# GpSimd sums the depthwise convolution's products four tiles at a time and completes conv_y itself, in a decoder trunk

## The chip, the cores and the metric

The kernel runs on one core of a Trainium2 chip (trn2). The metric is the device time of one execution, in microseconds; where several executions were timed, their median. PE is TensorE, DVE VectorE, ACT ScalarE, POOL GpSimd, SP SyncE.

## The reference, cut to what matters

One step of a two-layer trunk over 320 tokens (256 of a prompt, 8 samples of 8), with 2048 features. Layer 0 begins with a Conformer convolution module; it is the only part in which the change works on new data:

```python
def causal_dwconv(u, prev, w, bias):
    ext = jnp.concatenate([prev.astype(u.dtype), u], axis=1)
    y = lax.conv_general_dilated(ext, w[:, None, :].astype(u.dtype), window_strides=(1,), padding='VALID',
                                 dimension_numbers=('NWC', 'WIO', 'NWC'), feature_group_count=u.shape[-1])
    return y + bias, ext[:, -(w.shape[0] - 1):]

def conformer_conv(x, prev, w_in, b_in, w_dw, b_dw, g_n, b_n, w_out, b_out):
    a, gate = jnp.split(x @ w_in + b_in, 2, axis=-1)
    u = a * jax.nn.sigmoid(gate)
    u, new_prev = causal_dwconv(u, prev, w_dw, b_dw)
    u = jax.nn.silu(layer_norm(u, g_n, b_n))
    return u @ w_out + b_out, new_prev
```

The convolution has 31 taps per feature. Its result is normalised over the features, projected by w_out and added to DN_ALPHA * x. After it come a convolutional FFN, and in layer 1 window attention and another FFN; all of these are projections of the same kind.

## The kernel before, in words

Features lie on the 128 partitions, tokens on the free axis: x is xr[128, 16, 320]. Everything is float32. Each projection splits weights and activations into a high part (rounded to fp32r) and a low part, and sums three matmuls per 128x128 weight block: hi*hi, hi*lo, lo*hi (lines 377 to 379). Weights come by DMA from SP in half-groups ("chunks") of 128x1024 into four slots of w_raw, each as long as the longest chunk of a later stage (1408 columns); ScalarE rounds a chunk into w_hi (split_hi, line 685), VectorE writes w_lo = w_raw - w_hi (split_lo, line 991). A group is two chunks, 48 matmuls, and gives one feature tile of 128x320 in acc[0] or acc[1].

The w_in stage has 32 groups in 16 pairs ip; a pair gives the sigmoid input and the value of feature tile i. For each tile ScalarE takes the sigmoid (line 765), VectorE multiplies (gate, line 1093) into u_pad, ScalarE copies u_pad and the history into the overlapping segments u_seg (lines 783 to 785). Then the 31 taps are shared out: VectorE does 18 (lines 1102 to 1112), alternating between two PSUM banks sc[0] and sc[1]; ScalarE writes 13 products prods[:, n] (line 795), which GpSimd adds one by one into taps_pool, starting from minus the mean of tile 0 ("shift"; line 311). VectorE joins the three sums into conv_y (join, lines 1131 and 1133), but only in the next turn of the loop, after gate and the splits. For the last tile TensorE sums the products with an identity matmul (line 496), and ScalarE copies the sum to taps_pool (line 817). TensorE adds conv_y and its square (conv_square, line 708) to the moments of the norm (lines 466 and 472) two pairs late.

The order on each engine is the order of the code; all dependencies are semaphores written out by hand. ScalarE's turn is: sigmoid, four weight splits, wait for gate, u_seg, issue of the DMA that saves the state, 13 products (each waiting until GpSimd has taken the product of the tile before), a scaling of xr by ALPHA plus b_out (line 800), the square of the tile before. VectorE's turn is: two splits, gate, two splits, join of the tile before, 18 taps. SP's queue holds the weight loads, each waiting for the split of the chunk before in its slot. After tile 0 GpSimd issues three DMAs. In the norm that follows, GpSimd subtracts the mean from tiles 4 to 15 in three instructions of four tiles (center, line 329) while VectorE works on the others (lines 1021 and 1044). In the w_out stage VectorE adds the projection to xr (lines 1157, 1190 and 1196) and sums moments.

## Time and profile before

| | us |
|---|---|
| median of 3 runs | 2750.94 (2749.96 to 2757.99) |
| profiled execution: span | 2757.9 |
| the slowest of the three runs, beside that span | 2757.99 |
| TensorE busy in it | 2620.5 |
| VectorE, ScalarE, GpSimd busy | 1493.9, 1166.3, 274.9 |

The span is from the first to the last instruction of one profiled execution. Busy times of the other engines than TensorE are averages over very different stages; the w_in stage is the first 315 us, the w_out stage ends near 450 us. A row of the timeline gives the start, the duration (or, where equal instructions are merged, from the first start to the last end), the engine, the line, what is written and read, and in brackets the engine's idle time before it with the releaser.

### The profile page before, as it was taken

What the parts mean: (1) busy time and instruction counts of PE and PEld (TensorE: products, weight loads), DVE (VectorE), ACT (ScalarE), POOL (GpSimd) and SP (SyncE); (2) the same over time, 40 slices, a digit from 0 to 9 for tenths busy, and PEclk for the clock granted to TensorE, in tenths of its full rate; (3) what the DMA queues carried; (4) which work ended last, traced back from release to release, by engine and by line L of the source; (5) the groups of instructions that cost most, each with busy time, mean ns of one, the idle gap of its engine ahead of it and who ended that gap; (6) DMA issues with size and microseconds to landing.
All of it is one profiled execution on the core that took longest, in us unless ns stands there. A gap on an engine that the chain in (4) does not pass through costs nothing.

```text
span 2757.9 us, 48858 instructions
## 1 busy us (share of the span) xinstructions
PE 2620.5 (95%) x17562; PEld 2570.7 (93%) x17562; DVE 1493.9 (54%) x2187; ACT 1166.3 (42%) x1939; POOL 274.9 (10%) x224
## 2 busy tenths in 40 slices
PE   8889697999999999999989989899999999999996
PEld 7888597999999999999978979899999999999996
DVE  6888756544443344454466755654444334444555
ACT  7777635443332333343345433353343223443332
POOL 4888401000000000000010000100000000000001
PEclk9999798999999999999999968999999999999998
DMA  8444243444454344445433312434445434444542
GB/s 271 116 117 127 65 152 99 148 148 152 151 169 146 128 152 149 147 157 177 142 127 112 107 47 97 139 114 148 147 147 174 151 132 144 146 151 151 169 148 78
DMA packets 115061, 382.38 MB, mean 139 GB/s; under 512 B 29472, under 2 KB 29856, under 8 KB 114720
## 3 DMA queue, kind: packets, MB, share of 16 engines
q1 hardware_dynamic: 95328, 373.20, 41.4%
q0 software_dynamic: 992, 6.25, 0.6%
q10 hardware_dynamic: 18688, 2.21, 0.6%
q8 instruction: 34, 0.56, 0.1%
q14 instruction: 19, 0.16, 0.0%
HBM read 375.32 MB, written 8.27 MB: 139 GB/s over the span
## 4 chain that ended last, share of the span: by engine, by line
PE 85%; POOL 8%; DVE 3%; ACT 2%; issue 1%; POOLq 0%; DMA 0%; ACTq 0%; DVEq 0%; SPq 0%
PE acc L377 26%; PE acc L379 26%; PE acc L378 26%; POOL taps_pool L311 8%; PE acc L403 1%; PE acc L404 1%; PE acc L405 1%; DVE xr L1021 1%; ACT xr L728 1%; PE ot L665 0%; PE ot L667 0%; PE pt L564 0%; DVE rows L1034 0%; ACT xh L732 0%; PE pt L496 0%
## 5 line engine op out<-in xcount | busy, mean ns | idle before, releaser
L377 PE MATMUL acc<-xh,w_hi 128*128 128x320 f32 x3968 | 1236.1, 312 | 27.0 <-DVE w_lo L991 25.7
L379 PE MATMUL acc<-xh,w_lo 128*128 128x320 f32 x3968 | 1230.1, 310 | 0.0
L378 PE MATMUL acc<-xl,w_hi 128*128 128x320 f32 x3968 | 1229.7, 310 | 0.0
L685 ACT CAST w_hi<-w_raw 128x1024 fp32r<-128x1024 f32 (+1 forms) x648 | 699.0, 1117 | 556.2 <-PE acc L379 529.0
L991 DVE TENSOR_TENSOR w_lo<-w_raw,w_hi 128x1024 fp32r<-128x1024 f32 (+1 forms) x648 | 828.5, 1318 | 158.6 <-ACT w_hi L685 158.6
L377 PEld LDWEIGHTS acc<-xh,w_hi 128*128 128x128 f32 x3968 | 748.5, 189 | 41.9 <-DVE w_lo L991 32.4
L378 PEld LDWEIGHTS acc<-xl,w_hi 128*128 128x128 f32 x3968 | 748.6, 189 | 0.4
L379 PEld LDWEIGHTS acc<-xh,w_lo 128*128 128x128 f32 x3968 | 748.2, 189 | 0.0
L377 PE MATMUL acc<-hh,w_hi 128*128 128x320 f32 x1408 | 434.9, 309 | 0.0
L378 PE MATMUL acc<-hl,w_hi 128*128 128x320 f32 x1408 | 434.0, 308 | 0.0
L379 PE MATMUL acc<-hh,w_lo 128*128 128x320 f32 x1408 | 434.0, 308 | 0.0
L1157 DVE SCALAR_TENSOR_TENSOR xr<-xr,acc 128x320 f32 (+1 forms) x92 | 44.9, 488 | 417.0 <-PE acc L379 409.7
L378 PEld LDWEIGHTS acc<-hl,w_hi 128*128 128x128 f32 x1408 | 264.2, 188 | 0.3
L377 PEld LDWEIGHTS acc<-hh,w_hi 128*128 128x128 f32 x1408 | 264.2, 188 | 0.3
L379 PEld LDWEIGHTS acc<-hh,w_lo 128*128 128x128 f32 x1408 | 264.2, 188 | 0.0
L874 ACT ACTIVATE work<-acc,params 128x320 f32<-128x320 f32 x88 | 54.4, 618 | 376.1 <-PE acc L379 370.5
L311 POOL TENSOR_TENSOR taps_pool<-prods,taps_pool 128x320 f32<-128x320 f32 x180 | 208.7, 1159 | 25.8
L1237 DVE SCALAR_TENSOR_TENSOR work<-acc,params,work 128x255 f32<-128x255 f32 x88 | 42.5, 483 | 309.4 <-ACT ffn_out L878 309.4
L886 ACT CAST hh<-work 128x320 f32 (+1 forms) x88 | 40.4, 459 | 366.9 <-DVE work L1253 366.9
L1253 DVE TENSOR_TENSOR work<-work,acc 128x320 f32<-128x320 f32 x88 | 42.9, 488 | 184.4 <-PE acc L379 184.4
L403 PE MATMUL acc<-xh,w_hi 128*128 128x320 f32 x192 | 69.1, 360 | 62.1 <-DVE xl L1013 60.6
L1112 DVE SCALAR_TENSOR_TENSOR sc<-u_seg,params,sc 128x320 f32<-128x320 f32 x256 | 118.7, 547 | 0.0
(186 smaller groups left out, 1563.5 us busy)
## 6 DMA issues: line engine op xcount, KB each, us to landing
w_raw<-in_up SPq DMA_DIRECT2D x352, 512.0 KB, 4.3
w_raw<-in_down SPq DMA_DIRECT2D x128, 704.0 KB, 4.7
w_raw<-in_w_in SPq DMA_DIRECT2D x64, 512.0 KB, 5.9
w_raw<-in_w_out SPq DMA_DIRECT2D x32, 512.0 KB, 4.5
w_raw<-in_w_q SPq DMA_DIRECT2D x32, 512.0 KB, 4.8
w_raw<-in_w_o SPq DMA_DIRECT2D x32, 512.0 KB, 4.1
w_raw<-in_w_kv SPq DMA_DIRECT2D x8, 512.0 KB, 4.0
out_y<-xr SPq DMA_DIRECT2D x4, 640.0 KB, 3.0
```

Source lines behind the costliest of these rows:

```text
L311: pool.tensor_tensor(taps_pool[:, :], prods[:, n, :], taps_pool[:, :] if n else shift, ALU.add).then_inc(pool_taps, 1)
L377: pe.matmul(out, wh, hi[:, k, :], start=first, stop=False)
L378: pe.matmul(out, wh, lo[:, k, :], start=False, stop=False)
L379: mm = pe.matmul(out, wl, hi[:, k, :], start=False, stop=last)
L403: pe.matmul(out, wh, hi[:, k, :], start=(k == 0), stop=False)
L685: act.copy(w_hi[:, slot, 0:n], w_raw[:, slot, 0:n]).then_inc(hi_ready, 1)
L874: act.activation(work[:, 0, :], acc[0][:, 0:T], ACT.Identity, bias=par("f_b_dw")[:, tile, :], scale=taps[:, 2:3])
L991: dve.tensor_tensor(w_lo[:, slot, 0:n], w_raw[:, slot, 0:n], w_hi[:, slot, 0:n], ALU.subtract).then_inc(lo_ready, 1)
L1112: dve.scalar_tensor_tensor(dst, u_seg[:, :, tap:tap + SEG], w[:, tap:tap + 1], dst, ALU.mult, ALU.add).then_inc(dve_taps, 1)
L1157: dve.scalar_tensor_tensor(xr[:, k, :], xr[:, k, :], scale, acc[par_][:, 0:T], ALU.mult, ALU.add).then_inc(bank_read[par_], 1)
L1237: dve.scalar_tensor_tensor(gy[:, 1:SEQ], acc[0][:, 0:SEQ - 1], taps[:, 1:2], gy[:, 1:SEQ], ALU.mult, ALU.add).then_inc(taps_done, 1)
L1253: dve.tensor_tensor(work[:, 1, :], gy, acc[1][:, 0:T], ALU.mult).then_inc(bank_read[1], 1)
```

## The change

PARTS = 16: ScalarE makes 15 products, and the shift lies as sixteenth beside them (shift_part). GpSimd adds products 0 to 3 and 4 to 7 in one instruction of four tiles into parts, then 8 to 11 and 12 to 15 (with the shift), then folds four tiles to two and two to one, and adds that to conv_y, where VectorE has left its 16 taps. parts lies in columns of w_raw that the w_in stage doesn't use. ScalarE makes seven products at the end of tile i's turn and the other eight in the next turn, after the sigmoid and two splits. VectorE does its splits one by one between the taps and doesn't wait for GpSimd in the loop. SP saves the state. The scaling of xr goes to the w_out stage, where VectorE's instructions take ALPHA and b_out along. The scratch space of GpSimd's DMAs is set to 8192 bytes.

```diff
-POOL_TAPS = 13
-DVE_TAPS = CW - POOL_TAPS
+ACT_TAPS = 15
+PARTS = ACT_TAPS + 1
+EARLY_TAPS = 7
+POOL_STEPS = 5
+DVE_TAPS = CW - ACT_TAPS
+DVE_STEPS = DVE_TAPS + 1
+        parts = w_raw[:, :, KD // 2 * P:KD // 2 * P + T]
+        shift_part = prods[:, ACT_TAPS, :]
...
+            def save_state(i):
+                sp.wait_ge(useg_built, i + 1)
+                sp.dma_start(io["conv_state_out"][:, i], u_seg[:, PSEG - 1:NSEG, SEG:SEGW]).then_inc(state_saved, 16)
...
                 with sp.Fori(first, p.groups // 2) as ip:
                     load(p, ip, 0)
                     load(p, ip, 1)
+                    if p.base == 0:
+                        save_state(ip - 2)
...
-                for n in range(POOL_TAPS):
-                    pool.wait_ge(prod_ready, POOL_TAPS * i + n + 1)
-                    if n:
-                        pool.wait_ge(pool_taps, POOL_TAPS * i + n)
-                    pool.tensor_tensor(taps_pool[:, :], prods[:, n, :], taps_pool[:, :] if n else shift, ALU.add
-                                       ).then_inc(pool_taps, 1)
+            def conv_sum(i, first=False):
+                at = POOL_STEPS * i
+                pool.wait_ge(prod_ready, ACT_TAPS * i + 8)
+                if not first:
+                    pool.wait_ge(conv0_done, 1) if isinstance(i, int) else pool.wait_ge(shifted, i)
+                pool.tensor_tensor(parts, prods[:, 0:4, :], prods[:, 4:8, :], ALU.add).then_inc(pool_steps, 1)
+                pool.wait_ge(prod_ready, ACT_TAPS * i + 12)
+                pool.wait_ge(pool_steps, at + 1)
+                pool.tensor_tensor(parts, parts, prods[:, 8:12, :], ALU.add).then_inc(pool_steps, 1)
+                pool.wait_ge(prod_ready, ACT_TAPS * i + ACT_TAPS)
+                if not first:
+                    pool.wait_ge(shift_taken, 1)
+                pool.wait_ge(pool_steps, at + 2)
+                pool.tensor_tensor(parts, parts, prods[:, 12:16, :], ALU.add).then_inc(pool_steps, 1)
+                pool.wait_ge(pool_steps, at + 3)
+                pool.tensor_tensor(parts[:, 0:2, :], parts[:, 0:2, :], parts[:, 2:4, :], ALU.add
+                                   ).then_inc(pool_steps, 1)
+                pool.wait_ge(pool_steps, at + 4)
+                pool.tensor_tensor(parts[:, 0, :], parts[:, 0, :], parts[:, 1, :], ALU.add).then_inc(pool_steps, 1)
+                pool.wait_ge(pool_steps, at + 5)
+                pool.wait_ge(dve_taps, DVE_STEPS * (i + 1))
+                if not first:
+                    pool.wait_ge(shifted, i)
+                pool.tensor_tensor(conv_y[:, i, :], conv_y[:, i, :], parts[:, 0, :], ALU.add
+                                   ).then_inc(conv0_done if first else shifted, 1)
...
+            def products(i, taps, first=False):
+                for n in taps:
+                    if not first and n in (0, 8, 12):
+                        act.wait_ge(pool_steps, POOL_STEPS * (i - 1) + n // 4 + (n == 0))
+                    tap = DVE_TAPS + n
+                    act.activation(prods[:, n, :].rearrange("p (s q) -> p s q", q=SEG), u_seg[:, :, tap:tap + SEG],
+                                   ACT.Identity, scale=par("w_dw")[:, i, tap:tap + 1]).then_inc(prod_ready, 1)
...
                 split_next(p, i, 0, end, chunks=(1,) if first else (0, 1))
-                if not end:
-                    split_next(p, i, 1, end)
+                if not first:
+                    products(i - 1, range(EARLY_TAPS, ACT_TAPS), first=isinstance(i, int) and i == 1)
+                split_next(p, i, 1, end, chunks=(0,))
+                if not (isinstance(i, int) and i < 2):
+                    conv_square(i - 2, first=isinstance(i, int) and i == 2)
...
+                if not end:
+                    split_next(p, i, 1, end, chunks=(1,))
                 act.wait_ge(useg_built, i + 1)
-                act.dma_start(io["conv_state_out"][:, i], u_seg[:, PSEG - 1:NSEG, SEG:SEGW]).then_inc(state_saved, 16)
...
+                products(i, range(EARLY_TAPS), first)
...
-                act.activation(xr[:, i, :], xr[:, i, :], ACT.Identity, bias=par("b_out")[:, i, :], scale=ALPHA)
...
-            act.copy(taps_pool[:, :], pt[0][:, 0:T]).then_inc(sum_taken, 1)
...
+                if DVE_TAPS - 1 in taps:
+                    dve.wait_ge(dve_taps, steps + DVE_TAPS)
+                    dve.tensor_tensor(conv_y[:, i, :], conv_y[:, i, :], sc[0][:, 0:T], ALU.add).then_inc(dve_taps, 1)
...
+            def conv(i, end=False, first=False, find_shift=False):
+                split_next(p, i, 0, end, chunks=(1,) if first else (0, 1))
                 gate(i)
+                split_next(p, i, 1, end, chunks=(0,))
+                if find_shift:
...
+                conv_taps(i, range(6))
                 if not end:
-                    split_next(p, i, 1, end)
-                join(i - 1)
-                conv_taps(i)
+                    split_next(p, i, 1, end, chunks=(1,))
+                conv_taps(i, range(6, DVE_TAPS))
...
+            dve.wait_ge(shifted, KD - 1)
+            dve.wait_ge(dve_taps, DVE_STEPS * KD)
+            dve.wait_ge(products_summed, 1)
+            dve.tensor_tensor(conv_y[:, KD - 1, :], conv_y[:, KD - 1, :], pt[0][:, 0:T], ALU.add).then_inc(shifted, 1)
...
-                        dve.tensor_tensor(xr[:, k, :], xr[:, k, :], shift, ALU.subtract).then_inc(shifted, 1)
+                        if bias:
+                            dve.scalar_tensor_tensor(xr[:, k, :], xr[:, k, :], par(bias)[:, k, :], shift, ALU.add,
+                                                     ALU.subtract).then_inc(shifted, 1)
...
-            residual(ph["w_out"], 1.0, 1)
+            residual(ph["w_out"], ALPHA, 1, bias="b_out")
```

## Rows read from the trace of the kernel before

**Rows 1.** The page, part 4: the chain that ended last, by line.

```profile
PE acc L377 26%; PE acc L379 26%; PE acc L378 26%; POOL taps_pool L311 8%; PE acc L403 1%; PE acc L404 1%; PE acc L405 1%; DVE xr L1021 1%; ACT xr L728 1%; PE ot L665 0%; PE ot L667 0%; PE pt L564 0%; DVE rows L1034 0%; ACT xh L732 0%; PE pt L496 0%
```

**Rows 2.** Stretches: length, busy us (instructions) PE, PEld, DVE, ACT, POOL; clock, DMA, GB/s.

```profile
150.00:200.00 50.00, 45.49 (x289) 44.16 (x290) 41.05 (x67) 36.59 (x67) 41.20 (x36) 0.97 0.51 134
...
550.00:600.00 50.00, 50.00 (x343) 50.00 (x343) 24.37 (x35) 18.93 (x33) 0.00 (x0) 1.00 0.45 148
```

**Rows 3.** Timeline, GpSimd, in the w_in stage.

```profile
159.43 0.88 POOL L311 TENSOR_TENSOR taps_pool<-prods,rows 128x320 f32<-128x320 f32 x1 [1.40 <-DVE conv_y L1133]
160.46 15.75 POOL L311 TENSOR_TENSOR taps_pool<-prods,taps_pool 128x320 f32<-128x320 f32 x12
177.61 0.88 POOL L311 TENSOR_TENSOR taps_pool<-prods,rows 128x320 f32<-128x320 f32 x1 [1.40 <-DVE conv_y L1133]
```

**Rows 4.** Timeline, TensorE, the first matmul after a wait in the w_in stage.

```profile
150.54 0.41 PE L377 MATMUL acc<-xh,w_hi 128*128 128x320 f32 x1 [2.77 <-DVE w_lo L991]
```

**Rows 5.** Timeline in short windows, GpSimd: two single additions beside VectorE's subtractions.

```profile
149.42 2.93 POOL L311 TENSOR_TENSOR taps_pool<-prods,taps_pool 128x320 f32<-128x320 f32 x1
...
152.50 1.67 POOL L311 TENSOR_TENSOR taps_pool<-prods,taps_pool 128x320 f32<-128x320 f32 x1
```

**Rows 6.** Timeline in short windows, VectorE: two single weight subtractions.

```profile
150.41 1.22 DVE L991 TENSOR_TENSOR w_lo<-w_raw,w_hi 128x1024 fp32r<-128x1024 f32 x1
...
153.36 1.89 DVE L991 TENSOR_TENSOR w_lo<-w_raw,w_hi 128x1024 fp32r<-128x1024 f32 x1
```

**Rows 7.** Timeline, VectorE, one turn of the loop.

```profile
149.27 2.35 DVE L991 TENSOR_TENSOR w_lo<-w_raw,w_hi 128x1024 fp32r<-128x1024 f32 x2
151.54 0.54 DVE L1093 SCALAR_TENSOR_TENSOR u_pad<-acc,params,work 128x320 f32<-128x320 f32 x1
...
158.06 0.49 DVE L1131 TENSOR_TENSOR taps_pool<-sc,taps_pool 128x320 f32<-128x320 f32 x1 [2.82 <-POOL taps_pool L311]
...
159.12 0.60 DVE L1102 TENSOR_SCALAR sc<-u_seg,params 128x320 f32<-128x320 f32 x1
...
160.09 7.42 DVE L1112 SCALAR_TENSOR_TENSOR sc<-u_seg,params,sc 128x320 f32<-128x320 f32 x16
```

**Rows 8.** Timeline, GpSimd and then VectorE, in the norm after the w_in stage.

```profile
317.15 3.19 POOL L329 TENSOR_TENSOR conv_y<-conv_y,rows 128x1280 f32<-128x1280 f32 x1 [15.48 <-ACT rows L714]
...
317.15 6.28 POOL L329 TENSOR_TENSOR conv_y<-conv_y,rows 128x1280 f32<-128x1280 f32 x2 [15.48 <-ACT rows L714]
...
318.08 2.61 DVE L1021 TENSOR_TENSOR conv_y<-conv_y,rows 128x320 f32<-128x320 f32 x1
...
323.70 3.50 DVE L1021 TENSOR_TENSOR conv_y<-conv_y,rows 128x640 f32<-128x640 f32 x1
```

**Rows 9.** Timeline, ScalarE, one turn of the loop.

```profile
144.03 3.88 ACT L685 CAST w_hi<-w_raw 128x1024 fp32r<-128x1024 f32 x4
152.34 1.21 ACT L783 COPY u_seg<-u_pad 128x1216 f32<-128x1216 f32 x1 [4.43 <-DVE u_pad L1093]
...
153.75 0.24 ACT L785 COPY u_seg<-u_pad 128x64 f32<-128x64 f32 x1
...
154.78 6.32 ACT L795 ACTIVATE prods<-u_seg,params 128x320 f32<-128x320 f32 x13 [0.78 <-POOL taps_pool L311]
...
161.81 0.51 ACT L765 ACTIVATE work<-acc,params 128x320 f32<-128x320 f32 x1
```

**Rows 10.** Timeline, TensorE and then ScalarE, at the end of the w_in stage.

```profile
305.14 9.03 PE L496 MATMUL pt<-prods,consts 128*128 128x320 f32 x26
...
314.21 0.43 ACT L817 COPY taps_pool<-pt 128x320 f32<-128x320 f32 x1 [5.12 <-PE pt L496]
```

**Rows 11.** DMA issues: KB each, median us from issue to landing.

```profile
w_raw<-in_w_in SPq DMA_DIRECT2D x64, 512.0 KB, 5.9
...
out_conv_state_out<-u_seg ACTq DMA_DIRECT2D x16, 135.0 KB, 7.7
```

**Rows 12.** Groups by line and shape, from 100 to 290 us: busy, mean ns of one, idle before.

```profile
L991 DVE TENSOR_TENSOR w_lo<-w_raw,w_hi 128x1024 fp32r<-128x1024 f32 x41 | 57.9, 1452 | 0.0
```

More of the change, by code:

```diff
@@ L1094, in gate, with conv_taps @@
                                          ALU.add, ALU.mult).then_inc(bank_read[1], 1)
-            def conv_taps(i, first=False):
-                dve.wait_ge(useg_built, i + 1)
+            def conv_taps(i, taps):
                 sums = [b[:, 0:T].rearrange("p (s q) -> p s q", q=SEG) for b in sc]
                 w = par("w_dw")[:, i, :]
-                steps = DVE_TAPS * i
-                dve.tensor_scalar(sums[0], u_seg[:, :, 0:SEG], w[:, 0:1], par("b_dw")[:, i, :], ALU.mult, ALU.add
-                                  ).then_inc(dve_taps, 1)
-                if not first:
-                    dve.wait_ge(shifted, i)
-                dve.tensor_scalar(sums[1], u_seg[:, :, 1:1 + SEG], w[:, 1:2], None, ALU.mult).then_inc(dve_taps, 1)
-                for tap in range(2, DVE_TAPS):
-                    dst = sums[tap % 2]
-                    dve.wait_ge(dve_taps, steps + tap - 1)
-                    dve.scalar_tensor_tensor(dst, u_seg[:, :, tap:tap + SEG], w[:, tap:tap + 1], dst,
-                                             ALU.mult, ALU.add).then_inc(dve_taps, 1)
@@ L1135, in _ @@
-            split_next(p, 0, 0, False, chunks=(1,))
-            gate(0)
-            split_next(p, 0, 1, False)
-            conv_taps(0, first=True)
-            split_next(p, 1, 0, False)
-            gate(1)
-            join(0, conv0_done)
-            split_next(p, 1, 1, False)
-            dve.wait_ge(shift_ready, 1)
-            dve.tensor_scalar(shift, pt[0][:, 0:T], -1.0, None, ALU.mult).then_inc(shift_taken, 1)
-            dve.wait_ge(shift_taken, 1)
-            dve.tensor_tensor(conv_y[:, 0, :], conv_y[:, 0, :], shift, ALU.add).then_inc(shifted, 1)
@@ L1148, in _ @@
-            conv_taps(1)
-            pairs(p, conv, first=2)
-            join(KD - 1)
-            split_next(p, KD - 1, 1, True, chunks=(0,))
+                y = conv_y[:, i, :].rearrange("p (s q) -> p s q", q=SEG)
+                steps = DVE_STEPS * i
+                for tap in taps:
+                    if tap == 0:
+                        dve.wait_ge(useg_built, i + 1)
+                        if not (isinstance(i, int) and i == 0):
+                            dve.wait_ge(dve_taps, steps)
+                        dve.tensor_scalar(sums[0], u_seg[:, :, 0:SEG], w[:, 0:1], par("b_dw")[:, i, :],
+                                          ALU.mult, ALU.add).then_inc(dve_taps, 1)
+                    elif tap == 1:
+                        dve.tensor_scalar(sums[1], u_seg[:, :, 1:1 + SEG], w[:, 1:2], None, ALU.mult
+                                          ).then_inc(dve_taps, 1)
+                    else:
+                        dve.wait_ge(dve_taps, steps + tap - 1)
+                        dve.scalar_tensor_tensor(y if tap == DVE_TAPS - 1 else sums[tap % 2],
+                                                 u_seg[:, :, tap:tap + SEG], w[:, tap:tap + 1], sums[tap % 2],
+                                                 ALU.mult, ALU.add).then_inc(dve_taps, 1)
@@ L1152, in _ @@
+            conv(0, first=True)
+            conv(1)
+            conv(2, find_shift=True)
+            with dve.Fori(3, KD - 1) as i:
+                conv(i)
+            conv(KD - 1, end=True)
+            dve.wait_ge(shifted, KD - 1)
+            dve.wait_ge(dve_taps, DVE_STEPS * KD)
+            dve.wait_ge(products_summed, 1)
+            dve.tensor_tensor(conv_y[:, KD - 1, :], conv_y[:, KD - 1, :], pt[0][:, 0:T], ALU.add).then_inc(shifted, 1)
             norm(0, conv_y, after[p.name], RHS_CONV)
```

114 lines of the change are left out of this document (58 added, 56 removed).

## The prediction

> **What bounds it now.** I read the chain that ended last first. It is TensorE's matmuls almost everywhere, and for 8% of the span GpSimd's line 311 [rows 1]. Those additions stand only in the w_in stage, so there GpSimd sets the pace. The stretches show the same: with TensorE unhindered 343 matmuls start in 50 us, 0.146 us apart; in the w_in stage it is 289 [rows 2]. One turn of the loop over ip makes 96 such matmuls, 14.0 us, and two moments. GpSimd's first addition of a tile starts 18.18 us after that of the tile before [rows 3], and TensorE waits for w_lo between [rows 4].
>
> Of the 18.18 us, thirteen additions take 0.88 each with 0.14 between (160.46 less 159.43 less 0.88). The twelve that follow the first take 15.75 where 12.1 would do [rows 3]. The rest is three additions that last 2.93, 1.67 and a third like the second [rows 5]. Each stands beside a VectorE subtraction w_raw - w_hi, the one VectorE operation of the loop with two operands in SBUF. They take turns: the addition issued at 152.50 ended at 154.17, the subtraction issued at 153.36 ended at 155.25, 1.08 later [rows 5, 6]. The multiply-adds of the convolution (one operand in PSUM) run on undisturbed at 7.42/16 = 0.464 us [rows 7]. VectorE waits 2.82 us a turn for GpSimd before its join [rows 7].
>
> The norm shows the other side. GpSimd's additions of four tiles run from 317.15 to 320.34 and to 323.43. A VectorE subtraction of one tile, 0.49 us at join size [rows 7], issued at 318.08 lasts 2.61, and one of two tiles 3.50 [rows 8]. So VectorE waits to the end of a long GpSimd instruction. That decides here.
>
> **The change, part by part.** VectorE drops two taps and one join add, 2 x 0.46 + 0.49 = 1.4 us a turn, and its 2.82 us wait for GpSimd. ScalarE gets two products (2 x 6.32/13 = 0.97) and loses the xr scaling, an operation of the same size, and a DMA issue; it has 13 us free in 50 [rows 2, 9]. None of this is GpSimd's time, the bound.
>
> *GpSimd's work* becomes three additions of four tiles (A, B, C), one of two (D), two of one (E, F). The four-tile price: the norm's second one ended 3.09 us after the first, but VectorE's blocked subtraction ended between them, at 320.69 (318.08 + 2.61), and GpSimd ended 323.43 - 320.69 = 2.74 after that. An addition that had waited ended at 154.17, some 0.74 after the subtraction before it (which ended when the next was issued at 153.36, or up to 0.08 later) [rows 5, 6], 0.14 less than a free one, so a free four-tile addition is 2.9 us. Its bounds are 2.6 (3.09 less a whole VectorE addition of 0.49) and 3.5 (four times 0.88); I take 2.9 and, for the range, 3.12 beside it. Two tiles lie between 0.88 and 2.9 on a line: 1.56. The sum is 3 x 2.9 + 1.56 + 2 x 0.88 = 12.0, six gaps 0.8: 12.9, against 13 x 1.02 = 13.3 before. GpSimd gains 0.4 us by itself; what counts is where the subtractions meet additions three times as long.
>
> *The new loop, laid out by hand.* Zero is the moment when u_seg of a tile is ready. ScalarE: one split 0.97, seven products 3.40, sigmoid 0.5, two splits 1.94, the eighth product 0.5, signal 0.14 [rows 9]; GpSimd's first addition, A, which needs eight products, starts at 7.5 and ends at 10.4. VectorE: two first taps and four more 2.9, a subtraction 1.14, ten taps 4.64, the final add with its wait for the tap before 0.6 [rows 6, 7]: it asks for the first of the next pair's four subtractions at 9.3, while A runs. That ends at 10.4 + 1.08 = 11.5; B, waiting, goes before the second (as in rows 5 and 6) and ends 2.76 later, 14.25; the second subtraction ends at 15.35. Only now comes the gate, to 15.8, then 0.26 of signal and 1.65 of u_seg copies [rows 7, 9]: the next u_seg is ready at 17.7. **First kind of turn: 17.7 us.**
>
> In it, though, C runs until 15.35 + 2.76 = 18.1, and the third subtraction, asked for behind the gate at 15.75, ends at 19.2; the taps start 1.45 late. D, E, F run to 20.6, 21.6, 22.65; the fourth, among the taps, loses 0.55 to F. VectorE asks for its next pair at 19.2 + 2.85 + 0.55 + 1.1 + 5.2 = 28.9. A of that turn started at 17.7 + 7.5 = 25.2, ended at 28.1, and B has the port until 31.15. First subtraction 32.2, C until 35.0, second 36.1, gate 36.55, u_seg ready 38.45. **Second kind: 20.75 us.** In it D to F are soon out of the way (third subtraction ends at 38.6, fourth is free), so the first kind follows. The mean is 38.45/2 = 19.2 us, 1.05 above 18.18. GpSimd then idles for products: the loop runs through all three engines, with VectorE's wait for two long additions as its longest link.
>
> *How many turns.* GpSimd sums fifteen tiles; from the third on that is thirteen turns, 13 x 1.05 = 13.6 us. The start: A of tile 0 waits for the eighth product, now behind the next sigmoid, 7.3 us after u_seg by the layout, where the first product came 0.5 us after it: 0 to 7 us later than before. TensorE, which waits up to 2.77 us in a turn [rows 4], can catch much of it up. I take 0, as the thirteen turns already hold the first ones.
>
> *The end.* TensorE sums the last tile's products, 15 in place of 13: 9.03/13 = 0.69 each, so two more cost up to 1.4. ScalarE's copy (0.43) and one VectorE add (0.49) go with their signals, about 1.1 [rows 7, 10]. About zero.
>
> *Costs of nothing.* The state's DMA issue moves from ScalarE's queue to SP's, behind the pair's loads. Its wait, u_seg of a tile, was met before VectorE's later subtraction of that turn, for which the loads queued ahead of it waited, so it holds nothing up. It lands in 7.7 us and is wanted a turn later; the loads behind it land in 5.9, and each slot has some 10 us until its next split [rows 11]. If that cover went, a turn would grow by at most the excess, a few us. GpSimd's three DMA issues after tile 0 come later; their readers are stages away. Their smaller scratch has no row; should one of them wait for another to land, it is once, some 6 to 8 us [rows 11], in a queue that then idles for products: 0. In w_out ALPHA replaces 1.0 in the same instruction, the bias turns sixteen subtractions into multiply-add forms of the same size (0.46 against 0.49 [rows 7]), beside a TensorE that is full [rows 2]: 0 to 0.3 us.
>
> **Sum.** +13.6 + 0 + 0. The profiled execution (span 2757.9) is the slowest of the three runs shown, 2757.99, 7 us over their median; I add to the median: 2750.94 + 13.5 = 2764.4. With the bounds: 2.6 us for four tiles gives turns of 17.15 and 19.9, +5; 3.12 gives 18.1 and 21.4, +21. The forecast's own range is 2756 to 2775.
>
> **Rivals.**
> *GpSimd saturates and VectorE goes first: faster.* If GpSimd runs behind, A starts later than 9.3 after u_seg, right behind F of the tile before. Then VectorE's pair meets E and F (0.88) instead of A and B, the gate is early, the products are always ready. GpSimd's turn is 12.9 plus four subtractions at about 0.8 each (1.67 - 0.88, rows 5): 16.1, 2.05 below now; 13 turns give -27, a late start of up to 8 with nothing to hide it +8 to +10: -17, 2734. It feeds itself: what decides is whether A starts before or after VectorE asks, a margin of 9.3 - 7.5 = 1.8 us. For it: the first tiles are irregular and may fall into it; VectorE's unhindered pair got through before a waiting addition (issued 149.42, the second subtraction at 150.41, addition over at 152.35) [rows 5, 6]. Against: from the steady layout above nothing leads there.
> The Trainium skill ("SBUF — State Buffer", Who interferes with whom) says issue order decides and the loser blocks for the whole instruction; that speaks against this change, and the 3.50 us row agrees on the blocking [rows 8]. By its order alone that second subtraction should have waited behind the addition; the row has it the other way. By the rule's order this rival would be less likely still; the measurement decides, so it keeps its chance.
>
> *All turns of the first kind: no difference.* If the late taps are made good by shorter D to F, each turn is 17.7: -6, and 0 to +7 for the start: 2749.
>
> *All turns of the second kind: worse.* 20.75 each, +33: 2784. It takes VectorE 1 us later in every turn.
>
> **Chances.** Alternating turns 0.57; saturated 0.23; all first kind 0.15; all second kind 0.05. A measurement here can tell 0.3%, 8.3 us, from no change. Faster: the saturated case, 0.23. Same: the first-kind case and the forecast's lower end (0.05): 0.20. Slower: the rest, 0.57. Signs of both kinds hold much of the chance, so the range reaches from the middle of the saturated case to the top of the alternating one: 2733 to 2778.
>
> **What would show it.** Right: the subtraction of line 991, 1.45 us in the mean of the w_in stage [rows 12], becomes about 2.7 (by the layout 2.2, 3.9, 3.45, 1.75 and 3.3, 3.95, 2.1, 1.2 in the two kinds of turn); starts of GpSimd's four-tile additions come in threes with idle before the first, ended by ScalarE's products; turns alternate near 17.7 and 20.7; no join wait. Wrong: GpSimd busy without idle, turns near 16 and that mean near 2 (saturated); a free four-tile addition far from 2.9 us; or VectorE's subtractions not held by long additions.

## The result and the profile after

The changed kernel takes 2773.03 us in the median of four runs (2770.76 to 2775.22), against 2752.86 for the kernel before in the same comparison (four runs, 2749.96 to 2757.99). The ratio is 1.0069, with a 95% interval of 1.0054 to 1.0084: 20.2 us slower. The prediction said slower, 2764.4, in a range of 2733 to 2778. The direction held, and so did the turn of the loop that the prediction laid out. The increase was 13.5 in the prediction and 20.2 in the runs, its parts were shared out wrongly, and most of it remains when the conflict over reads, on which the prediction rested, is taken out of both kernels (experiment 1).

First the page of the changed kernel, busy times and the chain that ended last.

```profile
PE 2627.0 (95%) x17566; PEld 2572.5 (93%) x17566; DVE 1542.4 (56%) x2141; ACT 1172.4 (42%) x1954; POOL 276.8 (10%) x119
...
PE 87%; DVE 7%; issue 3%; ACT 2%; DMA 1%; POOL 0%; DVEq 0%; SPq 0%; ACTq 0%; POOLq 0%
PE acc L396 27%; PE acc L398 27%; PE acc L397 27%; DVE w_lo L1008 3%; DVE sc L1134 1%; PE acc L422 1%; PE acc L423 1%; PE acc L424 1%; DVE xr L1038 1%; ACT xr L746 1%; DMA out_conv_state_out<-u_seg 0%; PE ot L683 0%; PE ot L685 0%; PE pt L582 0%; DVE rows L1051 0%
```

GpSimd, 8% of the chain before [rows 1], is gone from it. VectorE's subtraction (line 1008) has come in with 3%, and its multiply-adds with 1%. GpSimd's busy time is the same as before (276.8 against 274.9), so the change didn't make it work less. Now the stretch that answers to the first of [rows 2], with the same columns, and the groups from 100 to 300 us that answer to [rows 12]:

```profile
150.00:200.00 50.00, 45.65 (x277) 42.97 (x276) 49.65 (x60) 34.82 (x64) 39.15 (x15) 0.93 0.39 113
```

```profile
L1008 DVE TENSOR_TENSOR w_lo<-w_raw,w_hi 128x1024 fp32r<-128x1024 f32 x43 | 116.1, 2718 | 0.0
...
L309 POOL TENSOR_TENSOR w_raw<-prods 128x1280 f32<-128x1280 f32 x10 | 29.6, 2961 | 30.2 <-ACT prods L788 30.2
```

TensorE starts 277 matmuls in these 50 us instead of 289, but in the next 50 it is 276 against 253: such a stretch cuts the turns at different places, and the turns have to be read from the timeline. VectorE shows 49.65 us busy of 50, but much of that is standing still inside an instruction: the same subtraction of 128x1024 took 1452 ns in the mean before and takes 2718 now. GpSimd, which must set the pace if its additions are the limit, waits 30.2 us in ten turns for ScalarE's products. The timeline of two turns, GpSimd and then VectorE, shows how that fits together:

```profile
153.35 2.97 POOL L309 TENSOR_TENSOR w_raw<-prods 128x1280 f32<-128x1280 f32 x1 [5.09 <-ACT prods L788]
...
170.82 2.96 POOL L309 TENSOR_TENSOR w_raw<-prods 128x1280 f32<-128x1280 f32 x1 [0.94 <-ACT prods L788]
173.85 2.89 POOL L312 TENSOR_TENSOR w_raw<-w_raw,prods 128x1280 f32<-128x1280 f32 x1
176.82 3.77 POOL L318 TENSOR_TENSOR w_raw<-w_raw,prods 128x1280 f32<-128x1280 f32 x1
180.67 2.42 POOL L320 TENSOR_TENSOR w_raw<-w_raw 128x640 f32<-128x640 f32 x1
...
191.22 2.97 POOL L309 TENSOR_TENSOR w_raw<-prods 128x1280 f32<-128x1280 f32 x1 [5.10 <-ACT prods L788]
...
174.16 3.66 DVE L1008 TENSOR_TENSOR w_lo<-w_raw,w_hi 128x1024 fp32r<-128x1024 f32 x1
...
177.75 3.93 DVE L1008 TENSOR_TENSOR w_lo<-w_raw,w_hi 128x1024 fp32r<-128x1024 f32 x1
181.59 0.54 DVE L1110 SCALAR_TENSOR_TENSOR u_pad<-acc,params,work 128x320 f32<-128x320 f32 x1
```

A, GpSimd's first addition of a tile, starts at 153.35, 170.82 and 191.22: one turn of 17.47 us, one of 20.40. This pair of turns repeats up to tile 13. In the second turn, VectorE asks for its two subtractions at 174.16, 0.31 after B (line 312) has started. It gets the first one done at 177.82, 1.08 after B's end; C (line 318), issued at 176.82, goes before the second, which ends at 181.68. Only then comes the gate (181.59), for which ScalarE waits with u_seg, and for ScalarE's products GpSimd waits 5.10 before the next A. In the first turn the pair is asked for while A runs, at 155.59, 2.24 after A's start, and is through 5.68 us later. That is the loop through three engines that the prediction laid out.

**Where the 20 us are.** The first additions of tiles 0, 1, 2 and 14 in the kernel before, and then in the changed one:

```profile
31.18 0.88 POOL L311 TENSOR_TENSOR taps_pool<-prods,rows 128x320 f32<-128x320 f32 x1 [30.72 <-ACT prods L795]
...
50.45 0.87 POOL L311 TENSOR_TENSOR taps_pool<-prods,rows 128x320 f32<-128x320 f32 x1 [2.78 <-ACT prods L795]
...
68.60 0.87 POOL L311 TENSOR_TENSOR taps_pool<-prods,rows 128x320 f32<-128x320 f32 x1 [1.41 <-ACT prods L795]
...
286.60 0.89 POOL L311 TENSOR_TENSOR taps_pool<-prods,rows 128x320 f32<-128x320 f32 x1 [1.40 <-DVE conv_y L1133]
```

```profile
37.85 2.98 POOL L309 TENSOR_TENSOR w_raw<-prods 128x1280 f32<-128x1280 f32 x1 [37.40 <-ACT prods L788]
...
55.11 2.94 POOL L309 TENSOR_TENSOR w_raw<-prods 128x1280 f32<-128x1280 f32 x1 [0.33 <-ACT prods L788]
...
77.56 2.97 POOL L309 TENSOR_TENSOR w_raw<-prods 128x1280 f32<-128x1280 f32 x1 [5.29 <-ACT prods L788]
...
284.43 2.95 POOL L309 TENSOR_TENSOR w_raw<-prods 128x1280 f32<-128x1280 f32 x1 [0.95 <-ACT prods L788]
...
308.63 3.55 POOL L309 TENSOR_TENSOR w_raw<-prods 128x1280 f32<-128x1280 f32 x1 [8.90 <-ACT prods L788]
...
336.38 9.37 POOL L348 TENSOR_TENSOR conv_y<-conv_y,rows 128x1280 f32<-128x1280 f32 x3 [13.63 <-ACT rows L732]
```

Up to tile 2, 77.56 against 68.60: +9.0. From there eleven turns to 284.43 last 18.81 in the mean, against (286.60 - 68.60)/12 = 18.17 before: +7.0. The last turn, to 308.63, lasts 24.20: +6.0. From there to the norm it is 27.75, against 317.15 [rows 8] less 286.60 = 30.55 before: -2.8. The sum, 19.2, is the whole difference at the norm. The spans of the two profiled executions end up only 15.5 apart (2773.4 less 2757.9). Up to the second norm, behind w_out, the changed kernel takes 1.5 less (131.73 against 133.24): behind the norm, for which TensorE had waited 11 us in both, its granted clock stands near the lower of its two levels (1.2 of 2.4 GHz) for 8.1 us in the kernel before (0.50 and, after one more wait, 0.54) and for 3.6 us in the changed one (0.51). The rest, 2.2, comes after the second norm, where the code is the same in all kernels of this document and where the profiled executions take anything from 2300.3 to 2307.6. So totals that differ by a few us, single runs above all, decide little, and the start of the norm in the trace is given beside them below.

Two waits on ScalarE belong to the odd turns:

```profile
68.73 1.21 ACT L814 COPY u_seg<-u_pad 128x1216 f32<-128x1216 f32 x1 [2.33 <-DMA out_conv_state_out<-u_seg]
...
305.78 1.05 ACT L703 CAST w_hi<-w_raw 128x1024 fp32r<-128x1024 f32 x1 [3.42 <-DMA w_raw<-in_w_out]
```

The first is the state of tile 1. In the chain that ended last (a row gives start, duration and what) its save is one long piece, 13.7 us where the prediction took 7.7:

```profile
54.84 13.72 DMA out_conv_state_out<-u_seg
```

The second is a weight load of the next stage that stands in SP's queue behind the save of tile 14, which waits for that tile's u_seg. To see how the 9.0 at tile 2 come about, here are the first sigmoid and tile 2's gate and u_seg, in the kernel before and then in the changed one (its u_seg is the first row above):

```profile
25.00 0.53 ACT L765 ACTIVATE work<-acc,params 128x320 f32<-128x320 f32 x1 [4.11 <-PE acc L405]
...
60.69 0.55 DVE L1093 SCALAR_TENSOR_TENSOR u_pad<-acc,params,work 128x320 f32<-128x320 f32 x1
...
61.99 1.21 ACT L783 COPY u_seg<-u_pad 128x1216 f32<-128x1216 f32 x1
```

```profile
25.66 0.53 ACT L793 ACTIVATE work<-acc,params 128x320 f32<-128x320 f32 x1 [4.49 <-PE acc L424]
...
63.30 0.54 DVE L1110 SCALAR_TENSOR_TENSOR u_pad<-acc,params,work 128x320 f32<-128x320 f32 x1
```

The first sigmoid comes 0.7 later, which chance can make: in the runs below, which are the changed kernel up to there (experiment 1 but for one bank set to zero), it comes anywhere from 23.49 to 25.93. From it the gate comes another 2.0 later, u_seg 4.1 more behind the gate (5.43 against 1.30; it waits for the save), and A 2.2 more behind u_seg (8.83 against 6.61; it waits for the eighth product, which ScalarE makes behind the next sigmoid). At tile 1 the delay was 4.7 (55.11 against 50.45), so the loop had caught up 2.0 before tile 2 lost it again.

### The profile page after: what moved, and what is told of

It reads as the page before. It is cut to its first block, busy times and chain, and to the rows that moved or that the text cites. A ratio compares the mean times of both kernels' runs of the same rounds, so it can differ in the third digit from the quotient of the medians.

```text
span 2773.4 us, 48282 instructions
## 1 busy us (share of the span) xinstructions
PE 2627.0 (95%) x17566; PEld 2572.5 (93%) x17566; DVE 1542.4 (56%) x2141; ACT 1172.4 (42%) x1954; POOL 276.8 (10%) x119
## 4 chain that ended last, share of the span: by engine, by line
PE 87%; DVE 7%; issue 3%; ACT 2%; DMA 1%; POOL 0%; DVEq 0%; SPq 0%; ACTq 0%; POOLq 0%
PE acc L396 27%; PE acc L398 27%; PE acc L397 27%; DVE w_lo L1008 3%; DVE sc L1134 1%; PE acc L422 1%; PE acc L423 1%; PE acc L424 1%; DVE xr L1038 1%; ACT xr L746 1%; DMA out_conv_state_out<-u_seg 0%; PE ot L683 0%; PE ot L685 0%; PE pt L582 0%; DVE rows L1051 0%
## 5 line engine op out<-in xcount | busy, mean ns | idle before, releaser
L1008 DVE TENSOR_TENSOR w_lo<-w_raw,w_hi 128x1024 fp32r<-128x1024 f32 (+1 forms) x648 | 898.3, 1424 | 163.5 <-ACT w_hi L703 163.4
L396 PEld LDWEIGHTS acc<-xh,w_hi 128*128 128x128 f32 x3968 | 750.9, 189 | 25.9 <-DVE w_lo L1008 13.2
L788 ACT ACTIVATE prods<-u_seg,params 128x320 f32<-128x320 f32 x240 | 117.8, 574 | 0.0
L348 POOL TENSOR_TENSOR xr<-xr,rows 128x1280 f32<-128x1280 f32 x12 | 37.5, 3148 | 764.1 <-ACT rows L732 764.1
```

The lines of the kernel that those rows point to most:

```text
L396: pe.matmul(out, wh, hi[:, k, :], start=first, stop=False)
L788: act.activation(prods[:, n, :].rearrange("p (s q) -> p s q", q=SEG), u_seg[:, :, tap:tap + SEG], ACT.Identity, scale=par("w_dw")[:, i, ta ...
L1008: dve.tensor_tensor(w_lo[:, slot, 0:n], w_raw[:, slot, 0:n], w_hi[:, slot, 0:n], ALU.subtract).then_inc(lo_ready, 1)
```

## Experiments

The diffs are against the changed kernel, unless said otherwise.

**1. Take the shared reads away.** In the w_in stage the subtraction reads its second operand from a PSUM bank of zeros. w_lo is then w_raw itself: the low part is left out, and what the kernel computes is no longer this step.

```diff
+                    if p.name == "w_in":
+                        halves = lambda t: t[:, slot, 0:n].rearrange("p (a b) -> p a b", a=2)
+                        zero = bass.AP(pt[1][:, :].tensor, pt[1][:, :].offset, [pt[1][:, :].ap[0], [0, 2], [1, 512]])
+                        dve.tensor_tensor(halves(w_lo), halves(w_raw), zero, ALU.subtract).then_inc(lo_ready, 1)
+                        continue
...
+            dve.memset(pt[1][:, :], 0.0).then_inc(zero_ready, 1)
+            dve.wait_ge(zero_ready, 3)
```

> Changed kernel, but in the w_in stage VectorE's weight split subtracts a PSUM bank of zeros in place of w_hi, so w_lo is there w_raw itself and not the low part; number, length and order of all instructions stay. Theory 1 (GpSimd's long additions hold up the subtractions that read two operands in SBUF, and this wait is the longest link of the loop): the subtraction falls from 2.72 us in the mean to 1.2 to 1.3, turns fall from 18.9 to about 15.6 (TensorE's own 15.1 and a little), time 2773 - 44 = 2729, 2722 to 2740. Rival 2 (the turn is set by ScalarE's new order: seven products, sigmoid, two splits, eighth product): subtractions get shorter, turns stay at 18 or more, time 2765 to 2773.

Measured: 2724.18 us, 49 less than the changed kernel. The same edit in the kernel before:

> Kernel before, with the w_in stage's weight split subtracting a PSUM bank of zeros in place of w_hi (w_lo there is not the low part). Theory 1 (the shared port costs the kernel before its turns too: 3.6 us of GpSimd's waits stand behind subtractions): GpSimd's turn would be 13 x 1.02 + 1.4 = 14.7, below TensorE's 15.1, so turns of 15.2 and 2752 - 39 = 2713, 2705 to 2722. Rival (GpSimd's own thirteen additions and the join set the turn): turns of 17 or more, 2735 or more.

Measured: 2713.59, 39 less than the kernel before. The groups from 100 to 300 us, and GpSimd's start in the norm, of the first run and of the second:

```profile
L1011 DVE TENSOR_TENSOR w_lo<-w_raw,pt 128x1024 fp32r<-128x1024 f32 x40 | 47.7, 1213 | 0.0
...
289.64 9.37 POOL L348 TENSOR_TENSOR conv_y<-conv_y,rows 128x1280 f32<-128x1280 f32 x3 [14.40 <-ACT rows L732]
```

```profile
L994 DVE TENSOR_TENSOR w_lo<-w_raw,pt 128x1024 fp32r<-128x1024 f32 x40 | 46.9, 1213 | 0.0
...
273.88 9.37 POOL L329 TENSOR_TENSOR conv_y<-conv_y,rows 128x1280 f32<-128x1280 f32 x3 [15.26 <-ACT rows L714]
```

In both the subtraction lasts 1213 ns. The turns are 15.6 us in the first; in the second they are 14.6 at first and 15.15 later, with TensorE busy all of the time from 150 to 200 us (50.00). ScalarE's order is the same in the first run as in the changed kernel, so that order alone doesn't make turns of 17.5 and 20.4 (rival 2); the shared reads do. But they cost the kernel before almost as much: 39 us of its total against 49, and 43.3 against 46.7 at the start of the norm. Without them the change is still slower, by 10.6 us in the totals of these two single runs and by 15.8 at the norm, where it is 19.2 with them. From tile 2 to tile 13 the turns are then 15.63 against 14.94 in the mean.

**2. Shorter instructions.** Each addition of four tiles becomes two of two.

```diff
-                pool.tensor_tensor(parts, prods[:, 0:4, :], prods[:, 4:8, :], ALU.add).then_inc(pool_steps, 1)
+                pool.tensor_tensor(parts[:, 0:2, :], prods[:, 0:2, :], prods[:, 4:6, :], ALU.add).then_inc(pool_steps, 1)
+                pool.tensor_tensor(parts[:, 2:4, :], prods[:, 2:4, :], prods[:, 6:8, :], ALU.add).then_inc(pool_steps, 1)
```

The other two additions are cut in the same way, and ScalarE's waits count the new steps.

> Changed kernel with each four-tile addition of GpSimd in two of two tiles. Theory 1: a subtraction waits for at most 1.6 us at a time; mean of the subtraction 1.85, turns about 16.6, time 2773 - 25 = 2748, 2742 to 2757, though GpSimd has three instructions more. Rival 2 (ScalarE's order): turns as before at 18.9, time 2773. Rival 3 (GpSimd's own work sets the turn): three more instructions of 0.1 to 0.15 us of fixed cost, turns 19.2, time 2777.

Measured: 2750.44 us. The group of the subtraction and two of the timeline's rows:

```profile
L1011 DVE TENSOR_TENSOR w_lo<-w_raw,w_hi 128x1024 fp32r<-128x1024 f32 x46 | 83.1, 1824 | 1.0 <-ACT w_hi L706 1.0
```

```profile
164.80 1.55 POOL L309 TENSOR_TENSOR w_raw<-prods 128x640 f32<-128x640 f32 x1
166.30 2.58 POOL L310 TENSOR_TENSOR w_raw<-prods 128x640 f32<-128x640 f32 x1
```

The same sum in halves gets 23 us back, to the time of the kernel before; the norm starts at 309.28, 7.9 before that of the kernel before, and the turns settle at 16.7. A two-tile addition takes 1.55 free, 2.58 where a subtraction comes in between.

**3. The other order.** From tile 2 on, A waits until VectorE has done the first subtraction of the next pair. That is the saturated rival, brought about by a wait that is added.

```diff
                 pool.wait_ge(prod_ready, ACT_TAPS * i + 8)
+                if not isinstance(i, int):
+                    pool.wait_ge(lo_ready, chunk(ph["w_in"], i + 2, 0, 0) + 1)
```

> Changed kernel; from tile 2 on GpSimd's first addition also waits until VectorE's first subtraction of the next pair is done. Theory 1: the pair of subtractions then goes through before the long additions, gate and u_seg come early; GpSimd gives up its idle time and saturates: turns about 16.2, mean of the subtraction 2.0, time 2773 - 27 = 2746, 2738 to 2756. Rival 3 (GpSimd's work sets the turn): each wait makes its first addition 3 to 4 us later, turns 21 or more, time 2795 or more.

Measured: 2740.81. The timeline of a turn, GpSimd and then VectorE:

```profile
161.27 3.75 POOL L311 TENSOR_TENSOR w_raw<-prods 128x1280 f32<-128x1280 f32 x1
...
172.97 1.58 POOL L322 TENSOR_TENSOR w_raw<-w_raw 128x640 f32<-128x640 f32 x1
174.63 0.88 POOL L325 TENSOR_TENSOR w_raw<-w_raw 128x320 f32<-128x320 f32 x1
175.86 1.46 POOL L331 TENSOR_TENSOR conv_y<-conv_y,w_raw 128x320 f32 x1 [0.34 <-POOL w_raw L325]
177.46 3.76 POOL L311 TENSOR_TENSOR w_raw<-prods 128x1280 f32<-128x1280 f32 x1
...
175.07 3.33 DVE L1010 TENSOR_TENSOR w_lo<-w_raw,w_hi 128x1024 fp32r<-128x1024 f32 x2
178.32 0.54 DVE L1112 SCALAR_TENSOR_TENSOR u_pad<-acc,params,work 128x320 f32<-128x320 f32 x1
```

VectorE's pair now meets E and F (0.88 us each when free) and is over in 3.33 us, where it took up to 7.5. The turn is 16.19 and GpSimd has no idle before A. A wait added to GpSimd made the kernel 32 us faster than the changed one (the norm starts at 302.29).

**4. Does one push do it?** Only tile 2's A waits; after it the loop is left to itself.

```diff
+                if isinstance(i, int) and i == 2:
+                    pool.wait_ge(lo_ready, chunk(ph["w_in"], i + 2, 0, 0) + 1)
...
             conv_sum(1)
-            with pool.Fori(2, KD - 1) as i:
+            conv_sum(2)
+            with pool.Fori(3, KD - 1) as i:
```

> Changed kernel; only tile 2's first addition waits for VectorE's first subtraction of the next pair, all later tiles run as in the changed kernel. Theory 1 with the prediction's remark that the saturated order feeds itself: the one push is enough, turns stay at 16.2 to the end, mean of the subtraction 2.05, time 2741, 2736 to 2748. If the saturated order has to be held by the wait in every turn: turns fall back to 17.4 and 20.4 after a few tiles, time 2760 to 2773.

Measured: 2768.2. A starts at 79.15, 94.61, 112.12 and 132.52, which is one turn of 15.5, then 17.5 and 20.4 again: the push is lost with the next tile. At tile 3, A started 1.5 us before VectorE asked for its pair (96.15). So one push is not enough. Which of the later waits are needed can be seen at A of tile 3, here, in experiment 3 and in the first run of experiment 8, which have the wait in every turn:

```profile
94.61 2.97 POOL L311 TENSOR_TENSOR w_raw<-prods 128x1280 f32<-128x1280 f32 x1
...
96.58 3.73 POOL L311 TENSOR_TENSOR w_raw<-prods 128x1280 f32<-128x1280 f32 x1 [0.15 <-POOL conv_y L331]
...
97.33 3.87 POOL L310 TENSOR_TENSOR w_raw<-prods 128x1280 f32<-128x1280 f32 x1 [2.72 <-DVE w_lo L1009]
```

In the third the wait holds A for 2.72 us, and the saturated order follows. In the second it holds nothing. From tile 4 on GpSimd has no idle before A in either, so the wait holds nothing there, which agrees with the prediction's "it feeds itself"; whether the order would last without the wait was not tried.

**5. The last turn.** The save of tile 14 goes behind the first loads of w_out.

```diff
                     load(p, 0, 1)
+                    save_state(KD - 2)
                     save_state(KD - 1)
...
-                if p.base == 0:
-                    save_state(KD - 2)
```

> Changed kernel with the save of tile 14's state behind the loads of w_out's first pair in SP's queue, in place of ahead of them. Theory 4 (SP, waiting for u_seg of tile 14, holds back w_out's first weights, and ScalarE's splits in the last turn wait for them): ScalarE's wait of 3.4 us for w_raw near 305 us goes, the last turn falls from 24.2 to about 20.4, time 2773 - 3.5 = 2769.5, with steady turns unchanged. Rival 5 (the loads are slow for lack of bandwidth at that time): the wait stays, time 2773.

Measured: 2769.39, 3.6 less, a single run. ScalarE's wait of 3.42 us is gone and the steady turns are as they were. In this run the turn before tile 3 was a short one (16.6), so that the last fell on 17.49; in the changed kernel it would have fallen on 20.4 (as it does in experiment 6), and the rest of its 24.20, some 3.8, is the wait. At the norm (330.38) this execution is 6.0 ahead of the changed kernel's; that includes the shorter last turn, and 1.2 by which its first sigmoid came earlier.

**6. The start, with the last turn mended.** GpSimd's three DMAs go behind its last tile, and VectorE takes the shift ahead of its pair in the third tile.

```diff
             conv_sum(0, first=True)
+            conv_sum(1)
+            with pool.Fori(2, KD - 1) as i:
+                conv_sum(i)
             pool.dma_start(ffn_in[:, :, :, :], io["ffn_state"][0]).then_inc(ffn_in_loaded, 16)
...
             def conv(i, end=False, first=False, find_shift=False):
-                split_next(p, i, 0, end, chunks=(1,) if first else (0, 1))
-                gate(i)
-                split_next(p, i, 1, end, chunks=(0,))
                 if find_shift:
...
+                split_next(p, i, 0, end, chunks=(1,) if first else (0, 1))
+                gate(i)
+                split_next(p, i, 1, end, chunks=(0,))
```

> The changed kernel with only its start and its end mended: the save of tile 14 after w_out's first loads, GpSimd's three DMAs after its last tile, and in VectorE's third tile the shift ahead of the pair's subtractions; nothing is left out and nothing in the loop's steady turns is touched. Theory (of the 20 us that the changed kernel is slower, some 9 are lost up to the third tile's A, 7 in eleven steady turns, 4 at the last turn through the save): the third tile's A starts 0.8 to 2.5 us earlier than 77.56 and no u_seg copy waits for a state's DMA; ScalarE's 3.4 us wait at the last turn is gone; steady turns stay at 17.5 and 20.4; time 2767 (2764 to 2770). Rival (the start's delay is caught up by the loop in any case): 2769.4, as with the late save alone. Second rival (the earlier shift tips the loop into the saturated order): turns near 16.2, 2740 to 2745.

Measured: 2771.35 in the median of four runs (2770.72 to 2772.4), 1.7 less than the changed kernel had in its own comparison. That is outside the expected 2764 to 2770, but by less than the comparisons differ: the kernel before took 2755.03 beside this run and 2752.86 beside the changed kernel. Three of A's starts in GpSimd's timeline, those of tiles 2, 13 and 14:

```profile
76.20 2.98 POOL L308 TENSOR_TENSOR w_raw<-prods 128x1280 f32<-128x1280 f32 x1 [6.76 <-ACT prods L787]
...
283.06 2.96 POOL L308 TENSOR_TENSOR w_raw<-prods 128x1280 f32<-128x1280 f32 x1 [0.97 <-ACT prods L787]
...
303.48 2.98 POOL L308 TENSOR_TENSOR w_raw<-prods 128x1280 f32<-128x1280 f32 x1 [5.09 <-ACT prods L787]
```

Tile 2 is 1.4 earlier than 77.56, but 1.0 of that is the first sigmoid, which came at 24.66, so the edits gave 0.4. No u_seg copy waits for a DMA. Instead C of tile 1, which no longer waits for the shift, now runs when VectorE asks for the pair of tile 2: the pair takes 6.42 us in place of 4.27, and the gate comes at 66.80. And the last A starts 2.0 later than in experiment 5 (301.47), because here the last turn falls on 20.42 and there on 17.49. Where turns of two lengths alternate, which of them comes last decides as much as such a gain at the start.

**7. The eighth product before the sigmoid.**

```diff
-EARLY_TAPS = 7
+EARLY_TAPS = 8
```

> ScalarE computes the eighth product before the next sigmoid and its two splits instead of after them, so GpSimd's first addition of a tile, A, can start some 0.7 us earlier after u_seg (one sigmoid of 0.5 and signals less), further ahead of VectorE's request for its pair; nothing is left out. Theory of the layout (the turn is a loop through all three engines, in which the eighth product's time stands ahead of A, B and the pair): each of the 13 turns loses at least those 0.7 us, and laid out step by step with A's earlier start the pattern becomes one of three turns, 19.1, 18.0 and 15.3 us, mean 17.5; the subtraction's mean falls from 2.72 to about 2.3; time 2754 (2748 to 2766). Rival (GpSimd's own work or ScalarE's products bound the turn): the turns stay at 17.5 and 20.4, time 2771 to 2775.

Measured: 2771.48 (2771.28 to 2772.58), at the rival's number, though not for the rival's reason: the turns are not 17.5 and 20.4, but all alike. GpSimd and then VectorE in the timeline:

```profile
73.03 2.97 POOL L309 TENSOR_TENSOR w_raw<-prods 128x1280 f32<-128x1280 f32 x1 [3.01 <-ACT prods L788]
...
242.78 2.97 POOL L309 TENSOR_TENSOR w_raw<-prods 128x1280 f32<-128x1280 f32 x1 [2.79 <-ACT prods L788]
247.09 2.89 POOL L312 TENSOR_TENSOR w_raw<-w_raw,prods 128x1280 f32<-128x1280 f32 x1 [1.33 <-ACT prods L788]
...
262.15 2.98 POOL L309 TENSOR_TENSOR w_raw<-prods 128x1280 f32<-128x1280 f32 x1 [2.78 <-ACT prods L788]
...
247.33 7.59 DVE L1008 TENSOR_TENSOR w_lo<-w_raw,w_hi 128x1024 fp32r<-128x1024 f32 x2
```

A third pattern, from tile 5 on every turn 19.4 us (262.15 less 242.78). A ends before VectorE asks, but B, which needs the twelfth product, waits 1.33 us and starts 0.24 before VectorE's request at 247.33. So the pair meets the whole of B and C in every turn. In the layout that was expected VectorE would have asked first; that this quarter of a microsecond decided it is argued and was not tried. The expectation also had the gain of A wrong: the product now stands before the two splits too, so A comes 2.3 earlier behind u_seg and not 0.7 (6.52 in place of 8.83 at tile 2, where u_seg starts at 66.51). Counted from the first sigmoid (24.78), A of tile 2 is 3.6 earlier than in the changed kernel; of the 4.5 between 77.56 and 73.03 the other 0.9 is the first sigmoid.

**8. A version that beats both.** Experiments 3 and 5 together, then with the start of 6, then with the eighth product early as well.

> VectorE first from tile 2 on, and the state of tile 14 saved behind w_out's first loads. Theories 1 and 4: the saturated order as before (turns 16.2); ScalarE's wait of 2.04 us for w_raw near 269 us goes, but in the saturated order GpSimd and not ScalarE sets the last turn, so 0 to 2 us: 2739, 2735 to 2743, against 2752 of the kernel before.

Measured: 2741.91 (four runs, 2737.47 to 2743.03), ratio to the kernel before 0.9961, interval 0.9946 to 0.9976.

> As the run before with VectorE first and the late save, and two edits of the start: GpSimd's three DMAs come after its last tile, and VectorE takes the shift ahead of the splits of its turn 2. Theory 6 (the start lost 9 us: the state of tile 1 lands late beside the cache copies, 1.8 to 2.3 us, and GpSimd's third addition of tile 1 waits 4.3 us for the shift that VectorE takes only behind four held subtractions): 2 to 5 us less than without, 2735, 2730 to 2740. If the start is set by tile 0's eighth product and additions alone: no change, 2739.

Measured: 2739.47 (five runs), ratio 0.9953, interval 0.994 to 0.9967, in the same comparison. A of tile 2 starts at 78.26, and C of tile 1 no longer waits for the shift, but A now waits 9.99 us there for VectorE's subtraction.

> The best version so far (VectorE's first subtraction of a pair ahead of A, and the start's and end's edits; 2739.5) with the eighth product before the sigmoid; nothing is left out. Theory (in that order GpSimd is saturated, and A waits for VectorE's subtraction and not for products): the eighth product is already there, steady turns stay at 16.2, time 2738 (2735 to 2741). Rival (products still hold A): turns and time fall by up to 0.7 x 13 = 9 us, 2730.

Measured: 2735.03 (four runs, 2732.36 to 2741.68), ratio 0.9928, interval 0.9912 to 0.9945, against 2755.03 for the kernel before beside it. The steady turns are still 16.18, so the products don't hold this order; nor does the subtraction in the steady turns, where GpSimd has no idle before A. The norm starts at 301.76, against 301.31 in the run before, so the trace shows no gain from the eighth product here. The time is 20 us less than that of the kernel before in the same comparison, and some 38 less than that of the changed kernel in its own.

## Why the prediction was right, and where its size was not

*Prices of GpSimd's additions: right.* Four tiles were taken at 2.9 us and take 2.89 to 2.97 free; two tiles at 1.56, 1.58 in experiment 1. "GpSimd gains 0.4 us by itself": where nothing interferes, from the first addition to the end of the last, it is 12.88 in experiment 1 against 13.18 in the same edit of the kernel before. The busy times of the pages, 276.8 and 274.9, can't show this, as they hold the blocked time too.

*The layout by hand: right.* Turns of 17.7 and 20.75 were forecast, 17.47 and 20.40 measured; the subtraction's mean 2.7, measured 2.718; the idle before A is ended by ScalarE's products and the wait for the join is gone. Experiments 1 to 3 show what sets the length of the changed kernel's turn, and not only its pattern: without the shared reads it falls to 15.6, and with the same work for each engine, halving the instruction gives 23 us back and reversing the order 32. The saturated rival was laid out at 16.1 per turn, and with the order forced it runs at 16.19. A starts 2.24 and 3.34 us before VectorE's request in the two turns (laid out as 1.8 in the first); that this margin, which the prediction named, keeps the kernel out of the saturated order agrees with experiments 3 and 4.

The Trainium skill ("SBUF — State Buffer", Who interferes with whom) says that a VectorE instruction with at most one input in SBUF, outside its two-port modes, does not contend with GpSimd; the 1213 ns of experiment 1 agree, being no more than the 1.22 us of an unhindered subtraction [rows 6]. It says too that issue order decides. In the changed kernel that holds for the rows above, where C, issued at 176.82, goes before the subtraction issued at 177.75; the second subtraction of an unhindered pair in the kernel before [rows 5, 6] still speaks the other way.

*"13 x 1.05 = 13.6 us": too large.* Both kinds of turn came out some 0.3 us shorter than laid out, and from A of tile 2 to A of tile 14 there are twelve turns, not thirteen. The eleven turns to tile 13 (six short ones, five long) gave 7.0; the last, without its 3.8 us of waiting, gives 20.4 less 18.17: 2.2. That is 9.2.

*"I take 0" for the start: wrong, 9.0.* This is the step that failed. Its reason was that TensorE can catch up and that the thirteen turns already hold the first ones. But the first A starts 6.7 us after the first addition of before (37.85 against 31.18), near the upper end of the 0 to 7 that the step itself gave. The delay was 4.7 at tile 1 and 9.0 at tile 2, and eleven steady turns make up none of it, as they are longer than before. At tile 2 the parts are the ones worked out above: 0.7 that chance can make, 2.0 at the gate, 4.1 for the save, 2.2 for the eighth product behind the sigmoid. Experiment 7 shows the last, the cause that the prediction named: with the product early, A comes 6.52 behind u_seg, as before the change (6.61). Experiment 6 takes u_seg's wait for the save away and gets 0.4, because the pair then meets C; so the parts do not add up when one is removed. What the 2.0 at the gate are was not settled.

*"Costs of nothing", SP's save: wrong, up to 4.1 and some 3.8 us.* "It holds nothing up" was argued for a steady turn, and there it is right. It fails at tile 2, where the save of tile 1 took 13.7 us to land instead of 7.7 and u_seg waited for it (2.33 us in the row, since ScalarE had stood at a square of tile 0 before), and in the last turn, where the save of tile 14 stands ahead of w_out's loads in SP's queue. Both are places outside the loop's steady state.

*The end, "about zero": -2.8,* more than the 1.1 that it gave as saved. In experiments 5 and 6, whose last turn has no wait, it is -1.6 and -1.8 (28.91 and 28.72 against 30.55), so some of the 3.8 waited in the last turn comes back here.

So the total has errors of both signs in it: the turns 4.4 too high and the end 2.8, the start 9.0 too low and the wait in the last turn 3.8; that is 5.6, the difference of the measured 19.2 and the 13.6. That the forecast's time lies only 8.6 us off the measured one is in part luck, as these errors have both signs.

And experiment 1, single runs in both kernels, shows that without the conflict of the two engines, on which the prediction rested alone, 15.8 of the 19.2 us at the norm remain (10.6 of 20.2 in the totals). So the conflict sets the turn of the changed kernel, but it is not shown to be why that kernel is slower than the one before, which paid almost as much for it. Of the 15.8, the way to tile 2 makes up 7.6 (71.72 against 64.08), the turns up to tile 14 10.0, and the end -1.8. What makes that start later was not tried.

## What to carry to other kernels

Merging small GpSimd additions into large ones saved 0.3 us of 13.2 a tile here, and it lengthens the time for which a VectorE instruction with two SBUF operands has to stand still, so look at which VectorE instruction falls on it and who waits behind that one, before counting busy times. Where both engines need the reads, the order in which they meet can be worth more than the work: a wait that lets the engine go first for whose result the loop is waiting paid here, and a single one at the loop's first tile was not enough. To say what a conflict costs a change, take it away in the kernel before too. Cost the first and the last turns of a loop on their own, by name, and not as part of the steady turn.

## What was not expected

The same loop has several stable patterns, with turns of 17.5 and 20.4, of 19.4, and of 16.2 us; a product that comes 2.3 us earlier changed the first into the second, and no gain was left. VectorE's busy time from 150 to 200 us says nothing of which kernel is near its limit: 49.65 of 50 us in the changed kernel, 49.90 in experiment 3, which is 32 us faster, and 41.58 in experiment 1, where more turns fall into the same stretch, since time held inside an instruction counts as busy.
